# Cross attention with values as stationary operand: the probabilities divided by their sums ahead of their transposes, the attended columns split straight from the banks

## What is computed

```python
def memory_cross_attention(hn, memn, wq, wkv, q_norm_g, k_norm_g, wo):
    q = rms_norm_2((hn @ wq).reshape(B, S, XATTN_HEADS, XATTN_HEAD_DIM), q_norm_g)
    k, v = jnp.split(memn @ wkv, 2, axis=-1)
    ...
    s = jnp.einsum('bshd,bmhd->bhsm', q, k).astype(jnp.float32) / math.sqrt(XATTN_HEAD_DIM)
    p = jax.nn.softmax(s, axis=-1)
    o = jnp.einsum('bhsm,bmhd->bshd', p.astype(v.dtype), v).reshape(B, S, D_MODEL)
    return o @ wo
```

## Time and profile before

| | |
|---|---|
| time, median of 3 runs | 1668.95 us (1668.63 to 1672.17) |
| the profiled execution | 1670.93 us, span 1669.1 us |
| mean granted clock of TensorE | 0.966 of full speed |
| PE / PEld busy | 88% / 49% of the span |
| DVE / ACT / POOL busy | 29% / 20% / 7% |
| the cross attention | about 1432 to 1481 us of the span |
| the MLP behind it | to 1669 us |

### The profile page before, as it was taken

One profiled execution on the slowest core, in us unless ns is written; L12 is line 12 of the kernel. 1 busy time (PEld: TensorE's weight loads), 2 busy tenths in 40 slices (PEclk: granted clock), 3 DMA queues, 4 the chain that ended last, 5 costly groups with the idle time before them and its releaser, 6 DMA issues. The chain is left out here.

```text
span 1669.1 us, 17593 instructions
## 1 busy us (share of the span) xinstructions
PE 1470.0 (88%) x7708; PEld 825.9 (49%) x7708; DVE 479.6 (29%) x728; ACT 339.9 (20%) x515; POOL 118.9 (7%) x113
## 2 busy tenths in 40 slices
PE   4999979889888899799798878878888999999999
PEld 2755642242242243299532323323324767788897
DVE  1487440100100000156500001001004754345443
ACT  1122410000000000134200000000003645544442
POOL 0000010000000000010100000000003044330000
PEclk9999989999989999999899999999999999999999
DMA  9989969999999999996499999999999844244510
GB/s 375 410 347 413 396 223 429 416 428 427 416 430 427 412 428 427 410 397 239 145 417 422 428 427 421 429 426 423 428 425 353 292 174 150 103 148 169 189 51 26
DMA packets 93298, 563.06 MB, mean 337 GB/s; under 512 B 8048, under 2 KB 9448, under 8 KB 53670
## 3 DMA queue, kind: packets, MB, share of 16 engines
q1 hardware_dynamic: 89504, 551.77, 81.2%
q0 software_dynamic: 2384, 9.42, 1.6%
q10 hardware_dynamic: 1334, 0.75, 0.2%
HBM read 558.74 MB, written 3.17 MB: 337 GB/s over the span
## 5 line engine op out<-in xcount | busy, mean ns | idle before, releaser
L2231 PE MATMUL ps<-ring,scratch 128*32 128x512 f32 x2048 | 432.5, 608 | 60.0 <-DMA ring<-in_moe_w_up 27.5
L2231 PEld LDWEIGHTS ps<-ring,scratch 128*32 128x32 f32 x2048 | 127.9, 112 | 351.6 <-issue 344.2
L2210 PE MATMUL ps<-ring,scratch 128*32 128x512 f32 x1024 | 205.3, 603 | 28.7 <-DMA ring<-in_moe_w_down 28.7
L1946 PE MATMUL ps<-ring_parts,scratch_parts 128*128 128x512 f32 x656 | 186.9, 403 | 5.0 <-DVE xT_parts L1208 1.4
L1946 PE MATMUL ps<-scratch_parts,ring_parts 128*128 128x256 f32 x704 | 146.1, 283 | 0.0
L1946 PEld LDWEIGHTS ps<-ring_parts,scratch_parts 128*128 128x128 f32 x656 | 122.6, 189 | 33.2 <-DVE xT_parts L1208 1.6
L2210 PEld LDWEIGHTS ps<-ring,scratch 128*32 128x32 f32 x1024 | 50.3, 111 | 159.2 <-issue 107.8
L614 ACT ACTIVATE ring_parts<-ring 128x2048 fp32r<-128x2048 f32 x56 | 106.4, 1919 | 93.1 <-PE ps L1946 86.5
L463 DVE TENSOR_TENSOR ring_parts<-ring,ring_parts 128x2048 fp32r<-128x2048 f32 x46 | 105.6, 2297 | 54.9 <-ACT ring_parts L614 53.9
L1946 PEld LDWEIGHTS ps<-scratch_parts,ring_parts 128*128 128x128 f32 x704 | 114.8, 189 | 0.3
L1534 DVE TENSOR_TENSOR scratch<-ps,gate_bc 128x512 f32<-128x512 f32 x16 | 11.1, 692 | 253.2 <-PE ps L2210 253.2
(11 more groups left out here) (393 smaller groups left out, 1565.1 us busy)
## 6 DMA issues: line engine op xcount, KB each, us to landing
ring<-in_moe_w_gate SPq DMA_DIRECT2D x64, 2048.0 KB, 30.0
ring<-in_moe_w_up SPq DMA_DIRECT2D x64, 2048.0 KB, 18.7
ring<-in_moe_w_down SPq DMA_DIRECT2D x64, 2048.0 KB, 30.2
ring<-in_ada_w SPq DMA_DIRECT2D x24, 2048.0 KB, 13.9
ring<-in_mlp_w SPq DMA_DIRECT2D x16, 2048.0 KB, 8.8
ring<-in_sc_w_in SPq DMA_DIRECT2D x6, 2048.0 KB, 21.7
ring<-in_w_in SPq DMA_DIRECT2D x6, 2048.0 KB, 20.3
ring<-in_xattn_wkv SPq DMA_DIRECT2D x4, 2048.0 KB, 35.5
```

Source lines behind the costliest of these rows:

```text
L1946: last = mm(out, lhs[x], rhs[y], start=start and n == 0, stop=stop and n == 2)
L2210: last = mm(ps[32 * j:32 * j + 32, banks[half], :], src[:, k, CAP * j:CAP * (j + 1)], w[:, e, col:col + 512], start=(k == 0), stop=(k == K ...
L2231: last = mm(ps[32 * j:32 * j + 32, banks[half], :], src[:, k, CAP * j:CAP * (j + 1)], w[e][:, 0, col:col + 512], start=(k == 0), stop=(k = ...
```

## The change

PE's values step takes 128 x 128 pieces of `xv` as the stationary operand and the transposed probabilities as the moving one. The result has the attended columns on the partitions and the tokens along the free dimension, which is the layout of the input columns of "wo". Rows can't be divided by their sums in this layout with one scalar per partition, so the probabilities are divided ahead of their transposes: VectorE takes the reciprocal of one unit's sums and scales `xp[:, n % 2]` in place (semaphore `xa_weights`), and the transposes wait for this instead of for the exponential. `attended_high` on ScalarE and `columns_low` on VectorE read the value banks directly. The transposes of attended rows and the multiplies by L1835 go. VectorE's order becomes: maximum of n, copy of n - 2, reciprocal and scaling of n - 1; in the second group's n = 5 `columns_low` stands ahead of the scaling of unit 4.

```diff
--- before.py
+++ after.py
@@ -972,6 +972,13 @@
                 nc.scalar.activation(xp[:, n % 2, :], ps[:, n % 2, 0:N], ACT.Exp, bias=sm[:, 64 + n:65 + n],
                                      scale=sm[:, 48 + n:49 + n], accum_out=sm[:, 96 + n:97 + n]).then_inc(sem("xa_p"), 1)
 
+            def attended_high(g):
+
+                for b in range(2):
+                    act.wait_ge(sem("xa_pv"), 4 * g + 2 * b + 2)
+                    k = 4 * g + 2 * b
+                    nc.scalar.activation(flat(x_hi[:, k:k + 2, :]), pb(XO[g] + b), ACT.Copy).then_inc(sem("x_high"), 1)
+
             xq_rows(0)
             high(FIRST["wo"])
             xq_columns(1)
@@ -980,13 +987,13 @@
             xq_rows(1)
             xq_columns(3)
             x_probs(4)
-            columns_high(16, (4, 5), x_hi)
+            attended_high(0)
             x_probs(5)
             high(FIRST["wo"] + 1, (0,))
             x_probs(6)
             x_probs(7)
             high(FIRST["wo"] + 1, (1,))
-            columns_high(18, (2, 3), x_hi[:, 4:8])
+            attended_high(1)
 
 
             high(mlp("up", 0))
@@ -1815,27 +1822,26 @@
                 dve.wait_ge(sem("cols_ps"), 12 + b + 1)
                 nc.vector.tensor_tensor(xqT[:, 2 * b:2 * b + 2, :], pb(XQT[b]).rearrange("p (k n) -> p k n", k=2),
                                         xqg.unsqueeze(2).broadcast_to([P, 2, N]), ALU.mult).then_inc(sem("cols"), 1)
-                for n in range(4 * g, 4 * g + 5):
+                for n in range(4 * g, 4 * g + 6):
                     if n < 4 * g + 4:
                         dve.wait_ge(sem("xa_s"), n + 1)
                         nc.vector.tensor_reduce(sm[:, 64 + n:65 + n], ps[:, n % 2, 0:N], AX.X, ALU.max, negate=True)\
                             .then_inc(sem("xa_max"), 1)
                     if g == 1 and n == 5:
                         columns_low("wo", 0, (4, 5), xT_r, x_hi)
-                    m = n - 1
+                    m = n - 2
                     if m >= 4 * g:
                         dve.wait_ge(sem("xa_pT_ps"), m + 1)
                         if m >= 2:
                             dve.wait_ge(sem("xa_pv"), m - 1)
                         nc.vector.tensor_copy(xpT[:, m % 2, :], pb(XPT[g] + m % 2)[:, 0:N]).then_inc(sem("xa_pT"), 1)
-                dve.wait_ge(sem("xa_pv"), 4 * g + 4)
-                link(nc.vector.reciprocal(sm[:, 112 + 4 * g:116 + 4 * g], sm[:, 96 + 4 * g:100 + 4 * g]))
-                for t in range(NT):
-                    r = sm[:, 112 + 4 * g:116 + 4 * g].rearrange("p (h t) -> p t h", t=NT)[:, t]
-                    nc.vector.tensor_tensor(rows[:, t, 512 * g:512 * g + 512].rearrange("p (h e) -> p h e", e=XD),
-                                            pb(XO[g] + t).rearrange("p (h e) -> p h e", e=XD),
-                                            r.unsqueeze(2).broadcast_to([P, 2, XD]), ALU.mult).then_inc(sem("xo"), 1)
-            columns_low("wo", 2, (2, 3), xT_r[:, 4:8], x_hi[:, 4:8])
+                    m = n - 1
+                    if 4 * g <= m < 4 * g + 4:
+                        dve.wait_ge(sem("xa_p"), m + 1)
+                        link(nc.vector.reciprocal(sm[:, 112 + m:113 + m], sm[:, 96 + m:97 + m]))
+                        nc.vector.tensor_scalar(xp[:, m % 2, :], xp[:, m % 2, :], sm[:, 112 + m:113 + m], None, ALU.mult)\
+                            .then_inc(sem("xa_weights"), 1)
+            columns_low("wo", 2, (6, 7), xT_r[:, 4:8], x_hi[:, 4:8])
             add_plain(3, "wo", (4, 5, 0, 1))
 
 
@@ -2555,7 +2561,7 @@
                 last.then_inc(sem("xa_s"), 1)
 
             def x_transposed(n):
-                pe.wait_ge(sem("xa_p"), n + 1)
+                pe.wait_ge(sem("xa_weights"), n + 1)
                 if n >= 2:
                     pe.wait_ge(sem("xa_pT"), n - 1)
                 for s in range(2):
@@ -2565,9 +2571,11 @@
             def x_values(n):
                 hd, t = n // NT, n % NT
                 pe.wait_ge(sem("xa_pT"), n + 1)
-                for s in range(2):
-                    last = mm(pb(XO[n // 4] + t)[:, XD * (hd % 2):XD * (hd % 2) + XD], xpT[:, n % 2, P * s:P * (s + 1)],
-                              xv[:, s, XD * hd:XD * (hd + 1)], start=(s == 0), stop=(s == 1))
+                for c in range(2):
+                    for s in range(2):
+                        last = mm(pb(XO[n // 4] + hd % 2)[:, N * c + P * t:N * c + P * (t + 1)],
+                                  xv[:, s, XD * hd + P * c:XD * hd + P * (c + 1)], xpT[:, n % 2, P * s:P * (s + 1)],
+                                  start=(s == 0), stop=(s == 1))
                 last.then_inc(sem("xa_pv"), 1)
 
             def wq_block(b):
@@ -2610,8 +2618,6 @@
             for n in range(4, 8):
                 if n == 4:
                     x_scores(5)
-                    pe.wait_ge(sem("xo"), 2)
-                    row_transposes(rows, (4, 5), range(0, 4))
                 elif n == 5:
                     pe.wait_ge(sem("x_split"), 4 * SPLIT_INPUTS.index("wo") + 2)
                     wo_block(0)
@@ -2632,9 +2638,6 @@
             x_values(7)
 
             for b in range(8):
-                if b == 4:
-                    pe.wait_ge(sem("xo"), 4)
-                    row_transposes(rows, (None, None, 2, 3), range(4, 8))
                 split_block(FIRST["wo"] + 1, 0, b // 4, b % 4, (x_hi, xT_r), b // 4)
             split_half(FIRST["wo"], 1, (x_hi, xT_r), (4, 5), waits=("wo", 2)).then_inc(sem("w_halves_used"), 2)
             split_half(FIRST["wo"] + 1, 1, (x_hi, xT_r), (0, 1), True).then_inc(sem("w_halves_used"), 1)
```

## The result

The changed kernel takes 1678.53 us (median of 5, 1677.42 to 1679.59), the kernel before 1669.27 us (5 runs, 1668.63 to 1672.17). The ratio is 1.0055, 95% interval 1.0044 to 1.0066: slower by 9.3 us in the medians. The forecast was slower by 4.5, range to 1676.0; the time lies 2.5 us above that range.

The account below looks back on a forecast made before the run. TensorE, busy 88% of the span, was taken as the bound, so attention losses arrive in full. Terms summed to +3.0 us, plus 1.5 for the clock: 4.5 on 1668.95 gives 1673.4 us, range 1670.0 to 1676.0.

Parts of the forecast that it names:

- T0: Transposes of unit 0's probabilities on PE, first group: wait for VectorE's maximum, reciprocal and scaling, 0.52 us later.
- T1, T2: Transposes of the probabilities of units 1 and 2: wait for VectorE's maximum, copy, reciprocal and scaling, 0.86 us lost each.
- T3: Transposes of unit 3's probabilities, last of the first group: VectorE's copy of unit 2 starts late, 0.34 us lost.
- start of S4: Scores of unit 4, first of the second group: start earlier without VectorE's row scaling ahead of them, -0.39 us.
- T4 and two blocks: Unit 4's probability transposes, then two wo blocks of three matmuls: wait for VectorE's subtractions, reciprocal and scaling, 0.65 us.
- T5: Transposes of unit 5's probabilities, second group: wait for VectorE's maximum, copy, reciprocal and scaling, 0.86 us lost.
- V7: Values step of unit 7, the last: four matmuls with 128 moving columns for two with 256, no added time.
- The clock: PE's granted clock falls to 0.50 around unit 4's transposes after a nearly idle stretch, costing 1.5 us.
- Rival A: The clock stays at 2.4 GHz through the attention: only +3.0 us, 1672.0 us; chance 0.24.
- B: Rival: VectorE's new work is ready before PE asks, so the waits vanish: -0.6 us, at best -1.3; chance 0.08.
- C: Rival: the 0.19 us weight load sets the pitch of the values matmuls: +8.1 us, 1677.1 us; chance 0.07.
- D: Rival: removed transposes and multiplies decide and the waits are half as long: +1.3 us, 1670.3 us; chance 0.11.

Follow-up runs that it names:

- e6b: The e2 kernel with 20 transposes, results unused, between the scores of unit 5 and the transposes of unit 4: 1672.91 us, ratio 1.0018.
- e6: The e2 kernel with 10 fp32r matmuls of 512 columns, results unused, between the scores of unit 5 and the transposes of unit 4: 1673.51 us, ratio 1.0017.
- e4: The changed kernel with 20 transposes, results unused, between the scores of unit 5 and the transposes of unit 4: 1680.20 us, ratio 1.0057.
- e8: The e7 kernel with the exponential written to SBUF and the scaling from SBUF to SBUF again: 1671.64 us, ratio 1.0009.
- e5: The e1 kernel with VectorE's reciprocal and scaling of n-1 moved ahead of the copy of n-2: 1674.37 us, ratio 1.0023.
- e2: The changed kernel with the exponential written in place to PSUM and VectorE's scaling reading it there: 1674.99 us, ratio 1.0029.
- e7: The e2 kernel reordered: scaling ahead of the copy, both blocks behind the next scores, column split and wo blocks moved into PE's gaps: 1665.61 us, ratio 0.9974.
- e1: The changed kernel with GpSimd's subtraction for half of the first wo chunk moved out of the first group's way: 1674.42 us, ratio 1.0021.
- e3: The changed kernel without reciprocal and scaling, so probabilities are not divided and transposes wait for the exponential: 1670.12 us, ratio 1.0000.

## Why the prediction was wrong

The step that failed is the price of the scaling: "The scaling, 128x256 f32 from SBUF to SBUF with a scalar per partition, is 0.349 in the nearest row; the bound above is the copy's 0.42." The row was right for an undisturbed instruction, and the bound was not a bound. The nearest rows, eight of L1593 (746.5 to 782.7 us), were taken where no instruction of GpSimd ran beside them; the copy that I took as the upper end reads a bank, and in the trace of before it took 0.42 us at 1436.40 with GpSimd's instruction beside it. That instruction stood over the very place where the first scaling would go, and I did not put the new instruction beside it:

```profile
1429.71 9.30 POOL L463 TENSOR_TENSOR ring_parts<-ring,ring_parts 128x2048 fp32r<-128x2048 f32 x2 [0.42 <-ACT ring_parts L614]
```

The trace of before also has a sign that the two engines can hold each other up. These two instructions of GpSimd have one form, and the first started while VectorE's L463, also from SBUF to SBUF, ran from 1356.16 to 1358.80:

```profile
1356.60 3.33 POOL L1132 TENSOR_TENSOR scratch<-scratch 128x512 f32<-128x512 f32 x1
1362.42 1.30 POOL L1132 TENSOR_TENSOR scratch<-scratch 128x512 f32<-128x512 f32 x1
```

Term by term, the end of each step against the kernel before, with the 0.34 us that the changed kernel was early at this point taken out:

| term | predicted | profile after |
|---|---|---|
| T0 | 0.52 | 3.24 |
| T1, T2 | 0.86 each | 0.83, 0.87 |
| T3 | 0.34 | 0.32 |
| start of S4 | -0.39 | -0.32 |
| T4 and two blocks | 0.65 | 0.63, and 0.86 of clock |
| T5 | 0.86 | 0.82, 0.52 of collision, 0.77 of clock |
| T6 | 0.16 | 0.18 |
| V7 | 0 | 0.07 |
| transposes, second group | -0.87 | -0.86 |
| sum | 3.0 + 1.5 | 7.9 |

The two scalings beside GpSimd cost 2.74 + 0.52 = 3.3 us that the sum lacked; with them it is 3.0 + 1.6 + 3.3 = 7.9. e6b, with neither collision nor fall, has a stage 4.0 above before: the predicted 3.0 and 7 x 0.13 = 0.9 for the slower scaling. So the queue of VectorE, the end of the T4 chain, the worth of both removed parts and the price of V held.

The clock: right in direction and size (1.63 us against 1.5), and e6 and e6b, with the gap filled, have no fall. That it came so close was partly luck. The reason for 1.5 and not 1.65, a fall begun before T4, did not come true: T4 took its 0.44 us, and the clock fell behind it. And the place was not certain: e4 and e8 had the fall behind T0, e5 behind T5, and in e2 it lasted twice as long. I had no term for a fall behind T0, since I had no 3 us wait there. Whether executions other than the profiled one had one stays open. The times don't ask for it: the medians differ by 9.3 us and the profiled executions by 7.6, but the profiled one of before was itself 1.7 above its median, and the interval of the ratio reaches from 7.3 to 11.0 us.

Rival A (the clock holds) fell, in the profiled execution. B (the new work is ready in time) fell for this order, and e7 shows what it asks for: 1.08 us of VectorE under 1.39 us of blocks. C fell with V at 0.89 to 0.90, though its 1677.1 us is the nearest of all to the measured time; that is chance, for the missing time lay elsewhere. D fell with the waits as long as forecast.

The missing term stands in the Trainium skill, where I did not weigh it. It says (SBUF — State Buffer, Who interferes with whom) that VectorE's tensor_scalar from SBUF to SBUF in its two-port mode and a GpSimd instruction exclude each other, and the later one waits for the whole of the earlier. The traces agree in eight places: 3.09 and 0.87 us (changed), 0.91 (e1), 3.09 and 2.49 (e4), 2.80 (e5), 3.51 and 1.59 (e8) for 0.35, each of them ending 0.14 to 0.15 us behind GpSimd's instruction. With the operand in PSUM all scalings of e2, e6, e6b and e7 took 0.48.

## What to carry to other kernels

When a change adds an instruction, lay it beside the other engines' timelines at the time when it will run; a duration from a quiet stretch is no upper bound. VectorE's fast form from SBUF to SBUF is a poor choice on the critical path beside long GpSimd instructions: reading the operand from the bank cost 0.13 us more each and took away up to 3.2. An edit that brings waits on a bound engine can still be worth making once the order covers them: here the same idea went from +0.55% to -0.26% with the order and one operand changed.

## What the runs showed of the hardware

- A VectorE tensor_scalar of 128x256 f32 from SBUF to SBUF took 0.35 us alone and up to 3.51 us beside a GpSimd tensor_tensor of 128x2048 (e8); from PSUM 0.48 us in either case (e2).
- The granted clock fell to 0.5 behind PE waits of 2.71 to 3.07 us (in e3 behind waits of 0.97, 0.67 and 1.37), but not behind each of them (T0's 3.02 in the changed kernel, T4's 2.94 in e5, T5's 2.75 in e4). One fall cost 1.63 us in the changed kernel and 1.69 in e3. With 20 transposes or 10 matmuls in the wait ahead of T4 no profile showed one there.
- f32 matmuls with 128 x 128 stationary and 128 moving columns follow one another in 0.11 us, loads included: 0.89 us for eight against 0.87 for four of 256 columns.
